# A two-layer attention block and a second block on one core: max rows as one-pass products, reciprocal spreads merged in pairs, and the second layer's context-key spread placed behind the third front tile

## The chip, the cores and the metric

The kernel runs on one core of one Trainium2 chip. The metric is the device time of one execution in microseconds (us); the median of three runs of the kernel before is 3325.97 us (3325.49 to 3326.18). Everything is float32 at the input and at the output.

## The reference, cut to what matters

Two blocks follow each other. The first (two layers, width 1024) has a main stream `x` of 512 tokens and a context stream of 256; the second block is left out here, since the change does not touch it.

```python
for l in range(2):
    zc = modulate(ctx_s, ...) @ w_in[l]
    qc, kc, vc = qkv_heads(zc, g_q[l], g_k[l])          # rms_norm over each head of 64
    z = modulate(x, ...) @ w_in[l]
    q, k, v = qkv_heads(z, g_q[l], g_k[l])
    q, k = apply_rope(q, cos, sin), apply_rope(k, cos, sin)
    k_all, v_all = concat(k, kc), concat(v, vc)         # 768 keys
    s = einsum(q, k_all) * 64 ** -0.5                   # 8 query heads, 2 key heads
    y_attn = softmax(s) @ v_all
    x = x + gt1 * merge_branches(z, y_conv, y_four, y_attn, ...)
    x = x + gt2 * sq_relu_mlp(...)
    if l == 0:                                          # the context's own attention, 256 keys
        yc_attn = gqa(qc, kc, vc); ctx_s = ctx_s + ...
```

In layer two the context stream is needed for its keys and values only.

## The kernel before, in words

**Weights.** Every weight comes from DRAM as a tile of 128 x 1024 float32 (512 KB) into one of four buffers `raw`, loaded by SyncE. ScalarE copies the tile into `w_hi` (type fp32r, L875), VectorE makes the rest `w_lo = raw - w_hi` (L2538). Both run three tiles ahead of TensorE (`LEAD`), with four buffers (`R`). On VectorE the making of `w_lo` for tile c + 3 stands in the same queue as the work on tile c, ahead of it (`lower_w` in `z_tile`).

**Products.** A product of full precision is three fp32r matmuls (`three`, L1644 to L1646: hi x hi, lo x hi, hi x lo). One front tile is 8 blocks of 3, so 24 matmuls of 128 x 512. A few small products have float32 operands instead of fp32r; each of these shows as two matmul records (and two weight loads) in the trace.

**Order.** The order of each engine's queue is the order of the code, written by hand; semaphores tie the engines together. The plan is: modulation, context stream of layer one (front, attention, merge, `w_o`, feed-forward), main stream of layer one, `kv_norm1` (keys and values of the context for layer two), main stream of layer two, then the second block.

**Max rows** (`max_row`, L1979). In an attention stage the largest score of each query is subtracted ahead of the exponential. VectorE reduces the scores of 128 queries to a column of 128 maxima, `mx` (L2839). For each head, TensorE turns these columns into one row with a product per 128 queries: weights are the column of `mx` (one column), moving is the identity of 128 columns; both are float32. A head has four such products in the main stream (512 queries) and two in the context stream (256). ScalarE reads the row (L1456), and the scores of the next head (`score_t`) wait for that. The stages have eight heads: the context of layer one, the main stream of layer one and that of layer two.

**Reciprocals** (`reciprocals_spread`, L2063). The denominators of the eight heads lie in rows 0, 32, 64 and 96 of two blocks of `scr`, four heads in each. In the merge stage each is spread over the 64 rows of its head: a float32 product with 64 weight columns for each head (a one at the head's row), two of them for the two halves of one bank. They are called in pairs of banks, behind merge tiles 0 and 1; so one call site issues four matmuls, with eight records. VectorE multiplies by each bank (L2915).

**Key norm of the context in layer two** (`kv_tail`). The context's keys are ready ahead of layer two's front. `front` first runs two tiles side by side (`abreast`), then `kv_tail`: sums of squares (L1811), the turned values (`v_turned`, L1765), and `head_spread` (L1792), which spreads the norm's factors over 128 rows and waits for them. These factors pass from ScalarE (root) to VectorE (reciprocal, L2673) and again to ScalarE (L1367, into `scr`). VectorE then multiplies the keys by the spread factors (L2684), copies them (L2690 to L2696), and goes on to the third front tile.

Of the kernel before, what the change touches and what calls it, by code (L numbers as in the profile page):

```python
# [7 lines left out]
F32R = mybir.dt.float32r  # L8
ALU = mybir.AluOpType
# [3 lines left out]
P = 128  # L13
# [3 lines left out]
CTX = 256  # L17
DEPTH = 2
HEAD = 64
# [364 lines left out]
def build(nc, ws, vecs, mats, ropes, x_in, ctx_in, bv_in, out, upto=None):  # L384
# [5 lines left out]
    with ExitStack() as stack:  # L390
        def sb(name, shape, dt=F32):
            return stack.enter_context(nc.sbuf_tensor(name, shape, dt))
# [15 lines left out]
        scr = sb("scr", [P, 4, SEQ])  # L408
# [4 lines left out]
        c_act = sb("c_act", [P, 16])  # L413
        c_parts = sb("c_parts", [P, KB, 4], F32R)
        pair = sb("pair", [4, 2])
        mx = sb("mx", [P, 2, 4])
        small = sb("small", [P, 64])
        eps = sb("eps", [P, 1])
        decay = sb("decay", [P, 4])
        unused_root = sb("unused_root", [P, 1])  # L420
        ones_r = sb("ones_r", [P, P], F32R)
        v_bias = sb("v_bias", [P, 8])
        o_bias = sb("o_bias", [P, 8])
        half_b = sb("half_b", [P, 8])
# [3 lines left out]
        bank = [stack.enter_context(nc.psum_tensor(f"bank{i}", [P, SEQ], F32)) for i in range(4, 8)]  # L428
        ring = stack.enter_context(nc.psum_tensor("ring", [P, R, SEQ], F32))

        ones, ident, head_ones, rot = (mat[:, i * P:(i + 1) * P] for i in range(4))
# [1207 lines left out]
        def _(pe):  # L1639
# [167 lines left out]
            def kv_tail(first):  # L1807

                pe.wait_ge(sq_ready, C.next(sq_ready))
                for tt in range(CTX // P):  # L1810
                    m = nc.tensor.matmul(bank[0][:, 2 * tt:2 * tt + 2], ctx_k_square[:, tt * P:(tt + 1) * P],  # L1811
                                         head_ones[:, 0:P:HEAD], start=True, stop=True)
                m.then_inc(ss_ready, 1)
                C.next(root_ready)
                v_turned("ctx", first + R)
                head_spread(0, CTX, False, 0, 0)
                C.next(lo_ready)

            def front(layer, stream, first):
                T, nf, main = length(stream), mix_tiles(stream), stream == "main"  # L1820
                k0, qn0, rot0 = C.now(lo_ready), C.now(s_qn) + (1 if layer else 0), C.now(s_rot_read)
                C.next(lo_ready, KB)

                def z_tile(c, before=None):
                    ready(c)
                    product(c, T, h_hi, h_lo, before=before)

                abreast(first, 2, T, k0)
                if layer:
                    kv_tail(first)  # L1830
                z_tile(first + 2)
                z_tile(first + 3)
                if layer:

                    pe.wait_ge(s_qn, C.next(s_qn))

                pe.wait_ge(lo_ready, C.next(lo_ready, 2))
                ready(first + 4)
                for tt in range(T // P):
                    s = slice(tt * P, (tt + 1) * P)  # L1840
                    for fb in range(2):
                        m = three(bank[tt][:, fb * 256:(fb + 1) * 256], y_hi[:, 2 + fb, s], y_lo[:, 2 + fb, s],
                                  *w(first + 4, 0, 256), True, True)
                m.then_inc(tile_done, 1)
                z_tile(first + 5)
                pe.wait_ge(lo_ready, C.next(lo_ready, T // P))
                half, nkt = T // 2, T // 2 // P
                per = TILE // half
                for parity in range(2):

                    at0 = parity * 2 * nkt
                    c = first + 6 + at0 // per
                    if at0 % per == 0:
                        ready(c)
                    for fb in range(2):
                        for idx in range(2 * nkt):
                            cs, kt = divmod(idx, nkt)
                            a = slice(fb * 256 + cs * P, fb * 256 + (cs + 1) * P)
                            b = 4 + parity * nkt + kt
                            m = three(bank[fb][:, parity * half:(parity + 1) * half], y_hi[:, b, a], y_lo[:, b, a],  # L1860
                                      *w(c, at0 % per + idx, half), idx == 0, idx == 2 * nkt - 1)
                    if parity or nf > 1:
                        m.then_inc(tile_done, 1)
                c = first + 6 + nf
                z_tile(c)

                pe.wait_ge(lo_ready, C.next(lo_ready, 2))
                head_sums(0, T)
                z_tile(c + 1)
                head_spread(0, T, main, qn0, rot0)  # L1870
                head_sums(1, T)
                z_tile(c + 2)
                head_spread(1, T, main, qn0, rot0)
                head_sums(2, T)
                z_tile(c + 3)
                head_spread(2, T, main, qn0, rot0)
                head_sums(3, T)
                z_tile(c + 4)
                head_spread(3, T, main, qn0, rot0)
                head_sums(4, T)  # L1880
                z_tile(c + 5)
                head_spread(4, T, main, qn0, rot0)
                z_tile(c + 6)
                z_tile(c + 7)
                C.next(s_qn, 5)

                pe.wait_ge(s_qn, C.now(s_qn))
                ready(c + 8)
                product(c + 8, T, h_hi, h_lo, o=bank[2][:, :T])

            def attention(layer, stream, first):
# [80 lines left out]
                def max_row(h):  # L1972

                    pe.wait_ge(s_max, C.next(s_max, nq))
                    if h >= 2:

                        pe.wait_ge(s_on, C.next(s_on, 2))
                    for qt in range(nq):
                        m = nc.tensor.matmul(bank[2 + h % 2][0:1, qt * P:(qt + 1) * P],  # L1979
                                             mx[:, h % 2, qt:qt + 1], ident, start=True, stop=True)  # L1980
                    m.then_inc(s_mrow, 1)

                def score_t(h, n):
# [74 lines left out]
            def reciprocals_spread(b, T):  # L2058
                if b % 2 == 0:
                    pe.wait_ge(s_recip, C.next(s_recip))  # L2060
                for i in range(2):
                    r = (2 * b + i) % 4 * 32
                    m = nc.tensor.matmul(bank[b][i * HEAD:(i + 1) * HEAD, :T],  # L2063
                                         ident[:, r:r + 1].to_broadcast([P, HEAD]), scr[:, 2 + b // 2, :T],
                                         start=True, stop=True)
                m.then_inc(s_spread, 1)

            def merge(stream, first):
                T = length(stream)
# [437 lines left out]
        def _(dve):  # L2507
            C = Counts()

            def step(ins, sem=dve_own):  # L2510

                ins.then_inc(sem, 1)
                dve.wait_ge(sem, C.next(sem))
# [1035 lines left out]
            dve.wait_ge(s_mat, 16)  # L3549
            step(nc.vector.tensor_tensor(pair[:, :], ident[0:4, 0:2], ident[0:4, 2:4], ALU.add), consts)  # L3550
            step(nc.vector.tensor_copy(ones_r[:, :], ones))

            dve.wait_ge(s_vec, 16)
            dve.wait_ge(s_lam, 1)
# [84 lines left out]
```

## Time and profile before

| what | value |
|---|---|
| median of three runs | 3325.97 us |
| time of the profiled execution | 3323.05 us |
| its span, first to last instruction | 3321.3 us |
| mean granted TensorE clock, as a share of 2.4 GHz | 0.987 |
| VectorE, ScalarE busy | 63%, 36% |
| moved from and to DRAM | 358 MB, mean 108 GB/s |
| the chain that ended last: TensorE, VectorE, ScalarE | 90%, 6%, 2% |

The span lies 1.75 us below the execution's own time; that execution lies 2.92 us below the median. A matmul record's duration contains latency that overlaps with the next matmul, so what a matmul costs is read from the distance between the starts of two that follow each other. In a row of the timeline the columns are: start in us, time in us that the merged instructions cover, engine, line, operation, output<-inputs, weights (rows*columns), output (rows x columns), count, and in brackets the engine's idle time ahead with what ended it.

### The profile page before, as it was taken

What the parts mean: (1) busy time and instruction counts of PE and PEld (TensorE: products, weight loads), DVE (VectorE), ACT (ScalarE), POOL (GpSimd) and SP (SyncE); (2) the same over time, 40 slices, a digit from 0 to 9 for tenths busy, and PEclk for the clock granted to TensorE, in tenths of its full rate; (3) what the DMA queues carried; (4) which work ended last, traced back from release to release, by engine and by line L of the source; (5) the groups of instructions that cost most, each with busy time, mean ns of one, the idle gap of its engine ahead of it and who ended that gap; (6) DMA issues with size and microseconds to landing.
All of it is one profiled execution on the core that took longest, in us unless ns stands there. A gap on an engine that the chain in (4) does not pass through costs nothing.

```text
span 3321.3 us, 43028 instructions
## 1 busy us (share of the span) xinstructions
PE 3239.8 (98%) x16209; PEld 2700.1 (81%) x16209; DVE 2096.4 (63%) x2914; ACT 1210.4 (36%) x1783; POOL 0.2 (0%) x4
## 2 busy tenths in 40 slices
PE   8999999999999999999999999999999999999998
PEld 5879997787888887878788888888888878888886
DVE  5777885655587778565466555785544576655446
ACT  3654444454232223344423222434222256542221
POOL 0000000000000000000000000000000000000000
PEclk9999999999999999999999999999999999999999
DMA  7554552211334454211122222231323336323222
GB/s 247 191 191 145 184 184 95 69 53 51 112 129 133 162 181 132 89 58 55 66 89 90 99 95 95 83 102 58 108 96 101 102 75 85 55 85 102 95 97 75
DMA packets 100717, 358.25 MB, mean 108 GB/s; under 512 B 11209, under 2 KB 12369, under 8 KB 100561
## 3 DMA queue, kind: packets, MB, share of 16 engines
q1 hardware_dynamic: 98864, 352.92, 31.9%
q10 hardware_dynamic: 1696, 3.16, 2.0%
q8 instruction: 109, 1.79, 0.2%
q14 instruction: 48, 0.39, 0.0%
HBM read 351.83 MB, written 2.10 MB: 107 GB/s over the span
## 4 chain that ended last, share of the span: by engine, by line
PE 90%; DVE 6%; ACT 2%; issue 1%; DMA 1%; DVEq 0%; ACTq 0%; SPq 0%
PE ring L1644 25%; PE ring L1645 25%; PE ring L1646 25%; PE bank L1644 2%; PE bank L1646 2%; PE bank L1645 2%; DVE w_lo L2538 1%; PE ring L1735 1%; ACT w_hi L875 1%; DMA raw<-ws 1%; PE ring L1968 1%; PE ring L1967 1%; PE bank L1992 1%; PE bank L1993 1%; PE ring L1938 1%
## 5 line engine op out<-in xcount | busy, mean ns | idle before, releaser
L1644 PE MATMUL ring<-h_hi,w_hi 128*128 128x512 f32 (+1 forms) x2776 | 1028.6, 371 | 21.1 <-DVE h_lo L2602 6.6
L1645 PE MATMUL ring<-h_lo,w_hi 128*128 128x512 f32 (+1 forms) x2776 | 1019.7, 367 | 0.0
L1646 PE MATMUL ring<-h_hi,w_lo 128*128 128x512 f32 (+1 forms) x2776 | 1019.3, 367 | 0.0
L2538 DVE TENSOR_TENSOR w_lo<-raw,w_hi 128x1024 fp32r<-128x1024 f32 x598 | 731.2, 1225 | 322.8 <-ACT w_hi L875 305.7
L875 ACT ACTIVATE w_hi<-raw 128x1024 fp32r<-128x1024 f32 x598 | 630.6, 1056 | 718.1 <-PE ring L1646 668.9
L1644 PEld LDWEIGHTS ring<-h_hi,w_hi 128*128 128x128 f32 x2776 | 528.8, 190 | 120.3 <-issue 28.5
L1646 PEld LDWEIGHTS ring<-h_hi,w_lo 128*128 128x128 f32 x2776 | 528.1, 190 | 86.0
L1645 PEld LDWEIGHTS ring<-h_lo,w_hi 128*128 128x128 f32 x2776 | 528.6, 190 | 82.4
L1644 PE MATMUL ring<-y_hi,w_hi 128*128 128x512 f32 (+1 forms) x1456 | 541.2, 372 | 10.4 <-DVE z L2817 7.8
L1645 PE MATMUL ring<-y_lo,w_hi 128*128 128x512 f32 (+1 forms) x1456 | 537.2, 369 | 0.0
L1646 PE MATMUL ring<-y_hi,w_lo 128*128 128x512 f32 (+1 forms) x1456 | 537.0, 369 | 0.0
L1644 PEld LDWEIGHTS ring<-y_hi,w_hi 128*128 128x128 f32 x1456 | 276.6, 190 | 60.4 <-DVE z L2817 10.7
L1646 PEld LDWEIGHTS ring<-y_hi,w_lo 128*128 128x128 f32 x1456 | 276.7, 190 | 45.8
L1645 PEld LDWEIGHTS ring<-y_lo,w_hi 128*128 128x128 f32 x1456 | 276.9, 190 | 44.2 <-issue 0.5
L1561 ACT ACTIVATE scr<-ring 128x512 f32<-128x512 f32 (+1 forms) x96 | 50.5, 526 | 302.5 <-PE ring L1646 300.0
L3033 DVE TENSOR_TENSOR z<-scr 128x512 f32<-128x512 f32 (+1 forms) x96 | 57.6, 600 | 125.1 <-ACT scr L1561 124.9
L2958 DVE SCALAR_TENSOR_TENSOR x<-ring,mod,x 128x512 f32<-128x512 f32 (+1 forms) x80 | 60.1, 751 | 118.3 <-PE ring L1646 118.2
L2849 DVE TENSOR_TENSOR y_lo<-z,y_hi 128x512 fp32r<-128x512 f32 (+1 forms) x112 | 72.3, 647 | 63.0 <-ACT y_hi L1472 61.6
L2839 DVE TENSOR_REDUCE mx<-ring 128x1 f32<-128x768 f32 (+1 forms) x80 | 67.9, 849 | 61.9 <-PE ring L1968 61.5
L1112 ACT ACTIVATE scr<-scr 128x512 f32<-128x512 f32 x40 | 25.3, 632 | 196.3 <-DVE scr L3326 196.3
L1472 ACT ACTIVATE y_hi<-bank 128x512 fp32r<-128x512 f32 (+1 forms) x112 | 63.4, 567 | 75.0 <-PE bank L1646 74.0
L1465 ACT ACTIVATE z<-bank 128x512 f32<-128x512 f32 (+1 forms) x112 | 63.6, 568 | 60.6 <-PE bank L1993 55.0
(369 smaller groups left out, 3136.8 us busy)
## 6 DMA issues: line engine op xcount, KB each, us to landing
raw<-ws SPq DMA_DIRECT2D x614, 512.0 KB, 3.3
z<-ws SPq DMA_DIRECT2D x48, 512.0 KB, 4.4
x<-x_t SPq DMA_DIRECT2D x1, 2048.0 KB, 12.1
out_t<-x SPq DMA_DIRECT2D x8, 256.0 KB, 2.0
z<-xc ACTq DMA_DIRECT2D x6, 256.0 KB, 11.3
xc<-ctx_t SPq DMA_DIRECT2D x1, 1024.0 KB, 7.7
z<-ropes ACTq DMA_DIRECT2D x2, 512.0 KB, 4.0
xc<-xc ACTq DMA_DIRECT2D x2, 256.0 KB, 11.2
```

The source lines that it names most:

```text
L875: nc.scalar.activation(w_hi[:, t % R, :], raw[:, t % R, :], ACT.Copy).then_inc(w_hi_ready, 1)
L1465: nc.scalar.activation(z[:, 13 + k % 2, :T], bank[k % 2][:, :T], ACT.Exp, scale=HEAD ** -0.5)\
L1472: nc.scalar.activation(y_hi[:, 4 + k % 2, :T], bank[k % 2][:, :T], ACT.Exp, scale=HEAD ** -0.5)\
L1561: nc.scalar.activation(scr[:, u % 2, :T], ring[:, c % R, :T], ACT.Relu).then_inc(evac, 1)
L1644: nc.tensor.matmul(o, a_hi, b_hi, start=start, stop=False)
L1645: nc.tensor.matmul(o, a_hi, b_lo, start=False, stop=False)
L1646: return nc.tensor.matmul(o, a_lo, b_hi, start=False, stop=stop)
L2538: nc.vector.tensor_tensor(w_lo[:, u, :], raw[:, u, :], f(w_hi[:, u, :]), ALU.subtract).then_inc(w_ready, 1)
L2839: nc.vector.reduce_max(mx[:, h % 2, qt:qt + 1], view[:, 0:n_kt * P], AX_X).then_inc(s_max, 1)
L2849: nc.vector.tensor_tensor(y_lo[:, b, :T], src, f(y_hi[:, b, :T]), ALU.subtract).then_inc(s_p, 1)
L2958: step(nc.vector.scalar_tensor_tensor(o, ring[:, c % R, :T], g, o, ALU.mult, ALU.add), post)
L3033: step(nc.vector.tensor_tensor(z[:, m % 2, :T], scr[:, m % 2, :T], scr[:, m % 2, :T], ALU.mult))
```

## The change

Three edits. First, `mx` is of type fp32r and is multiplied with an fp32r copy of the identity, `ident_r`. Second, a new constant `head_pick` has ones in 64 columns for each of the two heads of a bank, so that one product with 64 rows and 128 weight columns makes a whole bank: rows 0 to 63 for the even bank, rows 64 to 127 for the odd one. Third, `head_spread` leaves `kv_tail` and stands behind the third front tile of layer two. The two constants cost three VectorE instructions at the program's start.

```diff
-        mx = sb("mx", [P, 2, 4])
+        mx = sb("mx", [P, 2, 4], F32R)
...
+        ident_r = sb("ident_r", [P, P], F32R)
+        head_pick = sb("head_pick", [P, P])
...
                 v_turned("ctx", first + R)
-                head_spread(0, CTX, False, 0, 0)
                 C.next(lo_ready)
...
                 if layer:
                     kv_tail(first)
                 z_tile(first + 2)
+                if layer:
+                    head_spread(0, CTX, False, 0, 0)
                 z_tile(first + 3)
...
                         m = nc.tensor.matmul(bank[2 + h % 2][0:1, qt * P:(qt + 1) * P],
-                                             mx[:, h % 2, qt:qt + 1], ident, start=True, stop=True)
+                                             mx[:, h % 2, qt:qt + 1], ident_r[:, :], start=True, stop=True)
...
-                for i in range(2):
-                    r = (2 * b + i) % 4 * 32
-                    m = nc.tensor.matmul(bank[b][i * HEAD:(i + 1) * HEAD, :T],
-                                         ident[:, r:r + 1].to_broadcast([P, HEAD]), scr[:, 2 + b // 2, :T],
-                                         start=True, stop=True)
-                m.then_inc(s_spread, 1)
+                two = slice(b % 2 * HEAD, (b % 2 + 1) * HEAD)
+                nc.tensor.matmul(bank[b][:, :T], head_pick[two, :], scr[two, 2 + b // 2, :T],
+                                 start=True, stop=True).then_inc(s_spread, 1)
...
             step(nc.vector.tensor_copy(ones_r[:, :], ones))
+            step(nc.vector.tensor_copy(ident_r[:, :], ident))
+            for g in range(2):
+                step(nc.vector.tensor_tensor(head_pick[:, g * HEAD:(g + 1) * HEAD],
+                                             ident[:, 32 * g:32 * g + 1].to_broadcast([P, HEAD]),
+                                             ident[:, HEAD + 32 * g:HEAD + 32 * g + 1].to_broadcast([P, HEAD]), ALU.add))
```

TensorE's queue at the start of layer two's front, before. L1644 to L1646 are the matmuls of a product (behind the change L1646 to L1648), L1811 the sums of squares, L1765 the turned values, L1792 the spread.

```order
L1646 MATMUL ring<-h_hi,w_lo 128x512
L1811 MATMUL bank<-mat,z 128x2 x2
L1765 MATMUL bank<-mat,z 128x128 x2
L1792 MATMUL bank<-mat,scr 128x128 x2
L1644 MATMUL ring<-h_hi,w_hi 128x512
L1645 MATMUL ring<-h_lo,w_hi 128x512
```

The same place behind the change: the third tile's first matmuls follow the turned values.

```order
L1648 MATMUL ring<-h_hi,w_lo 128x512
L1813 MATMUL bank<-mat,z 128x2 x2
L1767 MATMUL bank<-mat,z 128x128 x2
L1646 MATMUL ring<-h_hi,w_hi 128x512
L1647 MATMUL ring<-h_lo,w_hi 128x512
```

And 24 rows on, where the third tile ends and the fourth begins, behind the change:

```order
L1647 MATMUL ring<-h_lo,w_hi 128x512
L1648 MATMUL ring<-h_hi,w_lo 128x512
L1794 MATMUL bank<-mat,scr 128x128 x2
L1646 MATMUL ring<-h_hi,w_hi 128x512
L1647 MATMUL ring<-h_lo,w_hi 128x512
```

The spread has moved behind the 24 matmuls of the third tile; nothing else of TensorE's queue moved there, and the queues of VectorE and ScalarE are the same as before at this place. TensorE's queue behind the first merge tile of layer one's main stream, before:

```order
L1645 MATMUL ring<-h_lo,w_hi 128x512
L1646 MATMUL ring<-h_hi,w_lo 128x512
L2063 MATMUL bank<-scr,mat 64x512 x4
L1644 MATMUL ring<-h_hi,w_hi 128x512
L1645 MATMUL ring<-h_lo,w_hi 128x512
```

and behind the change:

```order
L1647 MATMUL ring<-h_lo,w_hi 128x512
L1648 MATMUL ring<-h_hi,w_lo 128x512
L2065 MATMUL bank<-scr,head_pick 128x512 x2
L1646 MATMUL ring<-h_hi,w_hi 128x512
L1647 MATMUL ring<-h_lo,w_hi 128x512
```

Four products with 64 output rows became two with 128.

## Rows read from the trace of the kernel before

**Rows 1.** The page's first part: busy time, share of the span, instructions.
```profile
PE 3239.8 (98%) x16209; PEld 2700.1 (81%) x16209; DVE 2096.4 (63%) x2914; ACT 1210.4 (36%) x1783; POOL 0.2 (0%) x4
```

**Rows 2.** Timeline of TensorE, start of layer two's front.
```profile
1324.33 0.69 PE L1765 MATMUL bank<-mat,z 128*128 128x128 f32 x4
1330.01 1.23 PE L1792 MATMUL bank<-mat,scr 128*128 128x128 f32 x4 [4.99 <-ACT scr L1367]
...
1333.28 0.40 PE L1644 MATMUL ring<-h_hi,w_hi 128*128 128x512 f32 x1
...
1342.83 0.28 PE L1644 MATMUL bank<-w_hi,y_hi 128*128 128x256 f32 x1
...
1345.70 0.40 PE L1644 MATMUL ring<-h_hi,w_hi 128*128 128x512 f32 x1
```

**Rows 3.** Busy us by stretch (instructions), then granted clock, DMA share, GB/s.
```profile
108.00:245.00 137.00, 122.89 (x927) 106.82 (x927) 98.99 (x156) 82.55 (x147) 0.00 (x0) 0.95 0.60 202
640.00:760.00 120.00, 119.99 (x558) 96.31 (x558) 69.16 (x93) 58.78 (x96) 0.00 (x0) 1.00 0.16 53
1330.00:1333.00 3.00, 2.99 (x9) 2.60 (x10) 1.98 (x6) 1.17 (x2) 0.00 (x0) 0.52 0.12 44
```

**Rows 4.** Timeline of VectorE, the keys of the context in layer two.
```profile
1331.34 0.42 DVE L2684 TENSOR_TENSOR z<-z,bank 128x256 f32<-128x256 f32 x1 [0.66 <-PE bank L1792]
...
1334.28 1.23 DVE L2538 TENSOR_TENSOR w_lo<-raw,w_hi 128x1024 fp32r<-128x1024 f32 x1
```

**Rows 5.** Timeline of TensorE, first max row of layer one's main stream.
```profile
618.25 0.39 PE L1646 MATMUL ring<-h_hi,w_lo 128*128 128x512 f32 x1
618.57 1.03 PE L1979 MATMUL bank<-mat,mx 128*1 128x128 f32 x8
...
619.87 0.40 PE L1645 MATMUL ring<-h_lo,w_hi 128*128 128x512 f32 x1
```

**Rows 6.** Timeline of TensorE, short fp32r matmuls late in the program.
```profile
2749.78 0.22 PE L2363 MATMUL ring<-kv 128*128 128x128 f32 x1
2749.84 0.27 PE L2364 MATMUL ring<-kv 128*128 128x128 f32 x1
2749.95 0.45 PE L1644 MATMUL bank<-y_hi,w_hi 128*128 128x512 f32 x1
```

**Rows 7.** Timeline of TensorE, fp32r products with four weight columns begin.
```profile
124.24 0.28 PE L1646 MATMUL bank<-y_hi,kv 128*128 128x256 f32 x1
124.35 0.28 PE L1938 MATMUL ring<-w_hi,c_parts 128*4 128x256 f32 x1
```

**Rows 8.** Timeline of TensorE, first max row of the context stream.
```profile
109.80 0.60 PE L1979 MATMUL bank<-mat,mx 128*1 128x128 f32 x4
...
110.55 0.28 PE L1645 MATMUL ring<-h_lo,w_hi 128*128 128x256 f32 x1
```

**Rows 9.** Timeline of TensorE, float32 products with all 128 weight columns.
```profile
556.60 1.02 PE L1784 MATMUL bank<-z,mat 128*128 128x512 f32 x2
557.46 1.05 PE L1792 MATMUL bank<-mat,scr 128*128 128x128 f32 x8
558.35 0.51 PE L1772 MATMUL bank<-mat,scr 128*128 128x2 f32 x4
```

**Rows 10.** Timeline of TensorE, first reciprocals of layer one's main stream.
```profile
816.07 0.39 PE L1646 MATMUL ring<-h_hi,w_lo 128*128 128x512 f32 x1
816.39 1.94 PE L2063 MATMUL bank<-scr,mat 128*64 128x512 f32 x8
...
818.59 0.40 PE L1645 MATMUL ring<-h_lo,w_hi 128*128 128x512 f32 x1
```

**Rows 11.** Timeline of TensorE's weight loads, the same place.
```profile
816.87 0.14 PEld L2063 LDWEIGHTS bank<-scr,mat 128*64 128x64 f32 x2 [0.29 <-issue]
817.30 0.14 PEld L2063 LDWEIGHTS bank<-scr,mat 128*64 128x64 f32 x2 [0.28 <-issue]
```

**Rows 12.** Timeline of VectorE at the program's start.
```profile
26.14 1.22 DVE L2624 TENSOR_TENSOR z<-z 128x1024 f32<-128x1024 f32 x1 [9.69 <-ACT z L1319]
```

## The prediction

> **What bounds the kernel now.** I read the page's first part before anything else: TensorE is busy for 3239.8 of 3321.3 us, VectorE for 63%, ScalarE for 36% [rows 1]. So time is to be had in two ways: matmul time taken out where TensorE never rests, or an idle stretch of TensorE closed. The busy time by stretch then says which stage is which. From 640 to 760 us, inside the attention of layer one's main stream, TensorE is busy for 119.99 of 120 us at full clock while VectorE has 69 and ScalarE 59: there every us of matmul is a us of the kernel. From 108 to 245 us, the context's attention, it is busy for 122.9 of 137 us with VectorE at 99: there TensorE is only one of several links, and a part of what it saves is given back in waits [rows 3]. Last, the timeline at the start of layer two's front: an idle time of 4.99 us, TensorE waiting for ScalarE's copy of the key factors (L1367) [rows 2].
>
> **The third edit: the spread behind the third tile.** Before, the turned values start at 1324.33. Their four records are float32 with 128 columns, and eight such follow each other in 558.35 - 557.46 = 0.89 us, 0.11 each [rows 9]; so the third tile could start at 1324.77. What stands there instead is the spread at 1330.01, then the third and fourth tiles (48 matmuls, up to 1342.83) and the next tile's 24 matmuls of 256 columns, up to 1345.70 [rows 2]. From 1324.77 to 1345.70 is 20.93 us.
> After: the third tile waits for nothing that is late. The matmul at 1333.28 is the seventh of the 48, so the 42 steps to 1342.83 took 9.55, 0.2274 each; a tile at this pace is 5.46. The sum is 5.46 (third tile) + 0.45 (the spread, four records of 0.11) + 5.46 (fourth tile) + 2.87 (as now) = 14.24. Saved: 20.93 - 14.24 = 6.69. The idle time is 5.0 of it. The other 1.7 are a slow pace: between 1330 and 1333 the granted clock was 0.52 of 2.4 GHz, mostly the level of 1.2 GHz [rows 3], and before that TensorE had rested. With no rest there, I expect 2.4 GHz throughout.
> What is late next? The factors lie ready at about 1329.96 (the spread starts at 1330.01 [rows 2]), and the new spread starts at 1324.77 + 5.46 = 1330.23. So VectorE gets it at about 1331.4, as now (1331.34), and its `w_lo` for the tile three further on starts at 1334.28 as now [rows 4] and takes 1.23. TensorE then needs that `w_lo` at 1339.0 instead of 1345.7: slack 3.5 us. No DMA moves in SyncE's queue; the loads wait for `w_lo` and keep their times. I take 6.7. Bounds: 5.0, if only the idle time goes and the slow pace stays, and 6.9.
>
> **The first edit: max rows.** Main stream, before: from the start of the last ordinary matmul (618.25) to that of the second one behind the max row (619.87) are 1.62 us [rows 5]; two ordinary steps are 0.46, so a max row costs 1.16. Of that, eight records by 0.108 are 0.87, and 0.29 are gaps at the entry and the exit. After: four records, fp32r. The nearest rows are short fp32r matmuls of 128 columns, with 128 weight columns each: one follows 0.06 behind the other, and the next matmul 0.11 behind that, which is the pace at which such weights arrive [rows 6]. The weights here are one column, so I take 0.06, the pace of the moving columns: 4 x 0.06 = 0.24. As to the gaps: fp32r products with four weight columns begin 0.11 behind a 256-column matmul, without any gap [rows 7], and full-width float32 products begin without one too, the second group 0.86 behind the first for two records [rows 9]. The gap thus goes with float32 and few columns together, and should vanish. Saved: 1.16 - 0.24 = 0.92 for each of 8 heads x 2 stages, 14.7 us. Bounds: 0.64 each (10.2) with the gaps kept, 0.72 each (11.5) with 0.11 a record, 0.93 each (14.9) with 0.058.
> TensorEngine Tiling (Array Packing), section Tiling Modes, of the Trainium skill says that a change of tiling mode drains TensorE. By that rule a product of one weight column would be a tile of its own shape, fp32r or not, and the 0.29 would stay; rows 7 speak against it for fp32r.
> Context stream, before: 109.80 to 110.55 [rows 8], less two steps of 0.12, plus an entry gap of 0.09 as in rows 5, gives 0.60 to 0.72; for eight heads some 5.9 us (one of them runs at the half clock and costs 1.19). After: 2 x 0.06 each, with the slow one 1.0 in all. TensorE saves 4.9; as it idles for 14 of 137 us in this stage, waiting for chains over ScalarE and VectorE that in part start from TensorE's own tiles, I take 60%, 3.0. Bounds 0 and 4.9.
>
> **The second edit: reciprocals.** On paper two products become one. But the old ones already ran side by side. One full-width float32 product of 512 columns takes 0.86 for its two records, 0.43 each [rows 9]. Eight records of L2063 would be 3.4 us one after another; yet from 816.07 to 818.59 are 2.52, less 0.46 for two ordinary steps: 2.06, gaps of 0.34 included [rows 10]. The weight loads come in pairs 0.43 apart [rows 11]. So eight records took four steps of 0.43: the two halves of a bank, 64 columns each, shared the array.
> After, two products of 64 rows and 128 columns stand at a call, four records. In the array they lie in different rows, 0 to 63 and 64 to 127. If these share the array as the columns did, it is two steps: 0.86 + 0.34 = 1.20, saved 0.86. If not, four steps: saved nothing. There are four call sites in the main stream: 3.4 or 0. In the context (256 columns) half of it at two sites, 0.86, of which I keep 0.4, since the matmul behind it waits there for `w_lo` as well. I take 3.8: the nearest row, L2063 itself, shows that TensorE does run products on separate parts of the array at once. Bounds 0 and 4.3.
> TensorE: Matmul & The Clock Gate of the Trainium skill, section on packing small matmuls, gives 3.07x for four products of 32 rows each, so sharing by rows is a thing there; no row of this trace shows it. By the rule alone the term would be the same 3.4 to 4.3.
>
> **Start.** Three more VectorE instructions with fewer elements than the one of 0.42 us [rows 4], so under 1.3 us, are hidden by the 9.69 us that VectorE waits ahead of 26.14 [rows 12]. Cost 0; without that cover 1.3.
>
> **Sum.** 6.7 + 14.7 + 3.0 + 3.8 = 28.2. The profiled execution took 3323.05, 1.75 more than its span; 3323.05 - 28.2 = 3294.9. The median lies 2.92 higher: 3297.8, so 3298.
>
> **Rivals.**
> A. Products in separate rows do not run side by side. For it: no row shows rows sharing. Against: columns do. The second edit gives nothing: 24.4 saved, 3301.6.
> B. The gaps of the max row stay, because they belong to the one-column shape (the rule above), or a record costs 0.11. Against: rows 6 and 7. Main 10.2 to 11.5, context 1.5: 22.2 to 23.9 saved, 3302 to 3304.
> C. The chain binds in the context's attention, where a faster TensorE only waits longer; terms 3.0 and 0.4 go: 24.8 saved, 3301.2.
> D. Slower. The place is the two main attentions, the mechanism the clock. Each head's max row is now shorter, so TensorE comes earlier to products that wait for VectorE's or ScalarE's parts; a rest of some us went ahead of the 0.52 in rows 3. If such rests appeared once a head and left the clock at 1.2 GHz for half of the time, each us at that level would cost half a us. It decides from 2 x 28.2 = 56 us at the lower level; at 80 us of it the kernel would take 3298 + 40 = 3338. Against it: VectorE and ScalarE have half of their time free there, and TensorE rested for 0.01 of 120 us [rows 3].
>
> **How the numbers follow.** The forecast 0.62, A 0.16, B 0.09, C 0.09, D 0.02, and 0.02 for no change at all (the moved spread and the fp32r rows both hidden). The few stretches at the lower clock elsewhere may shift against the work by up to 3 us either way. Range: below, all terms at their best are 6.9 + 14.9 + 4.9 + 4.3 = 31.0, so 3295, less half of what the clock may give: 3293.5. Above, it holds A and C and most of B: 3304.5. A measurement of this kernel can tell about 0.2%, 6.7 us, from no change. Faster by more than that: 0.96; within: 0.02; slower: 0.02.
>
> **What would show it.** In the new profile: no wait of TensorE for L1367, the spread directly behind the third tile, and the granted clock at 1.0 from there. Max rows in four records 0.06 apart with no gap; if eight steps of time are still there or gaps of 0.1, B. Reciprocals: four records with two starts together and 0.43 between; four starts 0.43 apart, A. In the stretch of the context's attention, TensorE's idle time grows by less than 2 us; by 5, C. The forecast is wrong if the time lies above 3305 or below 3293.

## The result

The changed kernel takes 3295.53 us (median of four, 3294.24 to 3295.94); the kernel before, run beside it on the same chip, 3326.07 (3325.49 to 3328.72). The ratio is 0.991, interval 0.9898 to 0.9921: 30 us less, where 28.2 were worked out and 3298 was forecast. The profiled execution took 3295.76, its span 3294.0, against 3323.05 and 3321.3 before. So the two profiles are 27.3 us apart and the medians 30.5; the section on the reasons comes to that.

The page of the kernel after, first part, which answers to [rows 1]:

```profile
span 3294.0 us, 42823 instructions
PE 3215.2 (98%) x16105; PEld 2691.2 (82%) x16105; DVE 2096.2 (64%) x2917; ACT 1210.1 (37%) x1783; POOL 0.2 (0%) x4
```

TensorE lost 104 records (80 of the max rows, 24 of the reciprocals) and 24.6 us of busy time; the span fell by 27.3. Nothing else moved: VectorE has its three more instructions and the same busy time to 0.2 us.

**The spread.** Timeline of TensorE in the kernel after, the start of layer two's front, answering to [rows 2]:

```profile
1313.53 0.69 PE L1767 MATMUL bank<-mat,z 128*128 128x128 f32 x4
1313.98 0.48 PE L1646 MATMUL ring<-h_hi,w_hi 128*128 128x512 f32 x1
...
1319.52 0.60 PE L1794 MATMUL bank<-mat,scr 128*128 128x128 f32 x4
1319.88 0.48 PE L1646 MATMUL ring<-h_hi,w_hi 128*128 128x512 f32 x1
...
1325.41 0.28 PE L1646 MATMUL bank<-w_hi,y_hi 128*128 128x256 f32 x1
...
1328.29 0.40 PE L1646 MATMUL ring<-h_hi,w_hi 128*128 128x512 f32 x1
```

No idle time stands in it. The third tile starts 0.45 behind the turned values, the spread 5.54 later, the fourth tile 0.36 behind that, and the place that lay at 1345.70 lies at 1328.29. From the turned values to it are 14.76 us instead of 21.37: 6.6 less. Busy time by stretch, 22 us from the same point of the program on, first before, then after (columns as in [rows 3]):

```profile
1324.00:1346.00 22.00, 17.01 (x87) 14.63 (x86) 11.47 (x23) 7.65 (x14) 0.00 (x0) 0.92 0.32 106
```

```profile
1313.00:1335.00 22.00, 22.00 (x121) 19.10 (x120) 15.77 (x28) 11.71 (x20) 0.00 (x0) 1.00 0.41 139
```

The 5 us of rest are gone and the granted clock is 1.00 (2.4 GHz) in place of 0.92. VectorE has its turn a little earlier than forecast, answering to [rows 4]: 0.71 behind the spread's start, and 6.70 behind the start of the turned values, where 7.1 were forecast.

```profile
1320.23 0.42 DVE L2684 TENSOR_TENSOR z<-z,bank 128x256 f32<-128x256 f32 x1 [0.34 <-PE bank L1794]
```

**The max rows.** Timeline of TensorE after, the first max row of the main stream, answering to [rows 5]:

```profile
617.67 0.39 PE L1648 MATMUL ring<-h_hi,w_lo 128*128 128x512 f32 x1
617.90 0.40 PE L1982 MATMUL bank<-ident_r,mx 128*1 128x128 f32 x4
618.13 0.44 PE L1646 MATMUL ring<-h_hi,w_hi 128*128 128x512 f32 x1
618.41 0.40 PE L1647 MATMUL ring<-h_lo,w_hi 128*128 128x512 f32 x1
```

The row starts 0.23 behind a 512-column matmul, which is that matmul's ordinary step, so there is no gap at the entry; the next product starts 0.23 behind the row, so there is none at the exit. One thing is new: the product behind it takes a step of 0.28 instead of 0.23. By the same sum as before, 618.41 - 617.67 = 0.74, less two steps of 0.23, leaves 0.28 (0.29 in finer figures) for this row, which cost 1.16. Over the 16 rows of the two main stages, the same stretch takes 0.74 to 0.76 after and 1.62 to 1.63 before: 0.87 less for each.

**The reciprocals.** Timeline of TensorE after, the first call of the main stream, answering to [rows 10]:

```profile
808.45 0.39 PE L1648 MATMUL ring<-h_hi,w_lo 128*128 128x512 f32 x1
808.77 1.13 PE L2065 MATMUL bank<-scr,head_pick 64*128 64x512 f32 x4
809.83 0.50 PE L1646 MATMUL ring<-h_hi,w_hi 128*128 128x512 f32 x1
810.16 0.39 PE L1647 MATMUL ring<-h_lo,w_hi 128*128 128x512 f32 x1
```

810.16 - 808.45 = 1.71, less 0.46: 1.25, where it was 2.05. Four records of 0.43 one after another would be 1.72 alone, so the two halves of 64 rows do run at once. The four starts lie in pairs, as the records of L2065 in four short stretches show (length, busy time and, in brackets, the number of records in it, then clock, DMA share and GB/s):

```profile
808.76:808.79 0.03, 0.02 (x2) 1.00 0.00 0
808.79:809.29 0.50, 0.50 (x2) 1.00 0.31 82
809.29:809.32 0.03, 0.03 (x4) 1.00 0.00 0
```

Two records start within 0.03 us (at 808.768 and 808.775 in the trace), the other two start together 0.53 later. Before, the pairs of column halves followed each other 0.43 apart. The entry kept its gap: 0.32 from the matmul ahead to the first record, where that matmul's step is 0.23.

**The context's attention.** Busy time by stretch after, the stretches of [rows 3]:

```profile
108.00:245.00 137.00, 121.91 (x913) 109.33 (x912) 99.63 (x156) 82.87 (x147) 0.00 (x0) 0.93 0.61 202
630.00:750.00 120.00, 119.99 (x555) 98.53 (x554) 70.70 (x95) 61.70 (x101) 0.00 (x0) 1.00 0.17 57
```

In the main attention TensorE is as full as before. In the context's, though, the profile shows no gain at all: from the first max row to the first reciprocals are 134.94 us, and 135.06 before. The granted clock between 108 and 245 us was 0.93 in place of 0.95. That was the open question, and most experiments bear on it.

### The profile page after: what moved, and what is told of

It reads as the page before. It is cut to its first block, busy times and chain, and to the rows that moved or that the text cites. A ratio compares the mean times of both kernels' runs of the same rounds, so it can differ in the third digit from the quotient of the medians.

```text
span 3294.0 us, 42823 instructions
## 1 busy us (share of the span) xinstructions
PE 3215.2 (98%) x16105; PEld 2691.2 (82%) x16105; DVE 2096.2 (64%) x2917; ACT 1210.1 (37%) x1783; POOL 0.2 (0%) x4
## 4 chain that ended last, share of the span: by engine, by line
PE 90%; DVE 6%; ACT 2%; issue 1%; DMA 1%; DVEq 0%; ACTq 0%; SPq 0%
PE ring L1646 25%; PE ring L1648 25%; PE ring L1647 25%; PE bank L1646 2%; PE bank L1648 2%; PE bank L1647 2%; DVE w_lo L2538 1%; DMA raw<-ws 1%; ACT w_hi L877 1%; PE ring L1737 1%; PE ring L1971 1%; PE ring L1970 1%; PE bank L1995 1%; PE bank L1996 1%; PE ring L1941 1%
## 5 line engine op out<-in xcount | busy, mean ns | idle before, releaser
L1646 PE MATMUL ring<-h_hi,w_hi 128*128 128x512 f32 (+1 forms) x2776 | 1028.8, 371 | 21.9 <-DVE h_lo L2602 12.0
L1648 PE MATMUL ring<-h_hi,w_lo 128*128 128x512 f32 (+1 forms) x2776 | 1020.1, 367 | 0.0
L1646 PEld LDWEIGHTS ring<-h_hi,w_hi 128*128 128x128 f32 x2776 | 529.5, 191 | 116.0 <-issue 25.0
L1648 PEld LDWEIGHTS ring<-h_hi,w_lo 128*128 128x128 f32 x2776 | 529.1, 191 | 86.0
L1646 PE MATMUL ring<-y_hi,w_hi 128*128 128x512 f32 (+1 forms) x1456 | 540.0, 371 | 10.3 <-DVE z L2817 7.5
L1648 PE MATMUL ring<-y_hi,w_lo 128*128 128x512 f32 (+1 forms) x1456 | 536.5, 368 | 0.0
L1646 PEld LDWEIGHTS ring<-y_hi,w_hi 128*128 128x128 f32 x1456 | 275.9, 189 | 59.4 <-DVE z L2817 10.1
L1648 PEld LDWEIGHTS ring<-y_hi,w_lo 128*128 128x128 f32 x1456 | 275.7, 189 | 45.6
L2839 DVE TENSOR_REDUCE mx<-ring 128x1 fp32r<-128x768 f32 (+1 forms) x80 | 67.9, 849 | 62.0 <-PE ring L1971 61.5
```

Of the source, the lines that this page charges most:

```text
L1646: nc.tensor.matmul(o, a_hi, b_hi, start=start, stop=False)
L1648: return nc.tensor.matmul(o, a_lo, b_hi, start=False, stop=stop)
L2839: nc.vector.reduce_max(mx[:, h % 2, qt:qt + 1], view[:, 0:n_kt * P], AX_X).then_inc(s_max, 1)
```

## The experiments

The runs of each job share their own runs of the kernel before, with medians of 3324.34 (21 runs), 3325.00 (18) and 3325.12 (15).

The edits are shown shortened: arguments are left out (`...`), and so are the constants `ident_r` and `head_pick` with the VectorE instructions that make them, which each run has where it uses them.

**One edit at a time.** Each kernel is the one before with one of the three edits.

> The first edit alone (max rows in fp32r, the rest as before). My theory: in the main attentions the edit is worth 0.87 us for each of 16 heads, 13.9 us in all, and in the context's attention about nothing (the after trace shows TensorE there 1.7 us ahead and then back to 0.0). So the time is 3326 - 14 = 3312. Rival (the prediction's term): the context's attention gives 3 us more, 3309.

```
-   matmul(bank[2 + h % 2][0:1, ...], mx[:, h % 2, qt:qt + 1], ident)
+   matmul(bank[2 + h % 2][0:1, ...], mx[:, h % 2, qt:qt + 1], ident_r[:, :])   # mx in fp32r
```

Measured 3309.55 (3308.3 to 3311.09), ratio 0.9955 (0.9941 to 0.9968): 14.8 less. It is about half of the gain. That is nearer to the rival's 3309 than to the theory's 3312, but the interval (10.6 to 19.6 us) holds both.

> The second edit alone (one product of 64 rows for each bank). Theory: two products in rows 0 to 63 and 64 to 127 run side by side, 0.80 us saved at each of four main call sites, so 3.2 us, and with two sites in the context 3.6: 3322.4. Rival: they save nothing by themselves, and what the trace of the changed kernel gave there came from something else: 3326.

```
-   for two heads: matmul(bank[b][64 rows of it], mat, scr[...])
+   matmul(bank[b][:, :T], head_pick[two, :], scr[two, 2 + b // 2, :T])
```

Measured 3318.44 (3314.32 to 3323.1), ratio 0.9983 (0.9974 to 0.9992), 5.9 less by the medians. The call takes the same 1.25 us in its timeline as in the changed kernel. Four calls times 0.80 are 3.2, and the context's two calls 0.4 each at most; the interval (2.7 to 8.6 us) holds the 3.6 to 4.0, and the runs of this kernel are 8.8 us apart. In its profile, 5.2 us shorter than that of before, the four calls give 3.2, and two places where the clock stood low for less time give 1.6 each; the section on the reasons shows these two places.

> The third edit alone (the spread behind the third tile of layer two). Theory: the idle time of 5.0 us and the slow pace of 1.7 us behind it both go: 6.7 saved, 3319.3, and no half-clock stretch near 1330 us. Rival: only the idle time goes and the clock falls somewhere else: 3321.

```
-   head_spread(...); z_tile(first + 2); z_tile(first + 3)
+   z_tile(first + 2); head_spread(...); z_tile(first + 3)
```

Measured 3317.27 (3313.18 to 3323.77), ratio 0.998 (0.9971 to 0.9989): 7.1 less. The three alone make 14.8 + 5.9 + 7.1 = 27.8; together they gave 30. They add up within the scatter.

**Are the context's max rows worth anything?** The changed kernel with the old float32 rows in the context alone:

> The changed kernel, but the eight max rows of the context's attention are float32 products again (two records each); the 16 of the main streams stay fp32r. Theory: the context's attention is bound by chains and by stretches at the lower clock, so its eight faster rows give back nothing: as the changed kernel within 1 us, 3295.5. Rival: they are worth the predicted 3 us or more, and a clock stretch that fell badly hid it: 3298.5.

```
+   col = mx[:, h % 2, qt:qt + 1]
-   matmul(..., mx[:, h % 2, qt:qt + 1], ident_r[:, :])
+   matmul(..., col if main else col.bitcast(F32), ident_r[:, :] if main else ident)
```

Measured 3296.54 (3294.41 to 3299.34), ratio 0.9918 (0.9905 to 0.9932), against the changed kernel's 0.991. By the time alone they are one; that agrees with rows worth nothing, and with rows worth 3 as well. Its trace tells more: its stage took 134.84 us at a granted clock of 0.96, while the changed kernel had the same length at 0.92. I therefore ran both kernels again, to see what the clock does to this stage when the code is the same.

> The changed kernel once more, beside the others on one chip. Theory: what differs from one execution to the next is how long TensorE's clock stands at 1.2 GHz behind the same rests; in the context's attention the stage takes 132.5 us with 10 us at that level and 136.6 with 20. The sum of the times at the lower level and the span move together, half a us for each us. Rival: the stage takes 136.6 us whatever the clock.

Measured 3294.83 (3289.87 to 3296.87), ratio 0.991 (0.9895 to 0.9925).

> The kernel before once more, for a second profile. Theory: its context's attention takes 136.7 us with 10 to 14 us at the lower level and 140.6 with 20. Rival: 136.8 whatever the clock.

Measured 3326.31 (3323.2 to 3328.12), ratio 1.0 (0.999 to 1.001).

The same program, twice. Busy time by stretch of the changed kernel, first execution: from the first max row to the first reciprocals, and a part of it.

```profile
109.89:244.83 134.94, 119.85 (x895) 107.29 (x892) 97.77 (x153) 81.51 (x144) 0.00 (x0) 0.92 0.61 202
110.00:140.00 30.00, 24.84 (x173) 22.23 (x171) 19.70 (x33) 16.54 (x31) 0.00 (x0) 0.85 0.65 222
```

The same of its repeat:

```profile
109.06:239.80 130.74, 115.69 (x895) 103.35 (x892) 97.69 (x153) 81.29 (x144) 0.00 (x0) 0.96 0.63 208
110.00:140.00 30.00, 24.94 (x200) 21.97 (x200) 21.49 (x39) 17.66 (x31) 0.00 (x0) 1.00 0.67 226
```

The number of TensorE's records is the same, 895, and the stage is 4.2 us shorter. Between 110 and 140 us the engine was busy for as long (24.84 and 24.94), but did 173 records in one execution and 200 in the other, because in the first a part of them ran at 1.2 GHz. Both executions rest at the same place (next fences), so the rest goes before the low clock in one of them and doesn't in the other. The repeat of the changed kernel, TensorE's timeline:

```profile
117.23 0.39 PE L1970 MATMUL ring<-kv,y_hi 128*128 128x256 f32 x1 [3.39 <-DVE y_lo L2791]
```

and its first execution:

```profile
118.24 0.58 PE L1970 MATMUL ring<-kv,y_hi 128*128 128x256 f32 x1 [3.56 <-DVE y_lo L2791]
```

The matmul behind the rest takes 0.58 at the one level and 0.39 at the other. With this, each run's stage can be set beside its clock. From the first max row to the first reciprocals, in us, for every profile without filling matmuls; each column has the granted clock of that stretch and, from the trace's record of the granted level, the us at 1.2 GHz in it:

| context's rows | 0.96 (10.2 us) | 0.95 (13.7 us) | 0.94 (17.1 us) | 0.93 to 0.92 (20.5 us) |
|---|---|---|---|---|
| float32 | 134.79, 134.84 | 135.06 (before) | 137.23, 137.97 (before, again) | 138.84, 137.78 (128 weight columns) |
| fp32r | 130.74 (changed, again), 131.06 (128 weight columns) | | | 134.94 (after), 134.81, 135.25 |

With rows of one weight column, the two kinds are 134.8 and 130.7 at 0.96, and 138.8 (one execution) and 135.0 at the low end: the fp32r rows save 3.8 to 4.1 us of this stage at either clock, and 10.3 us more at 1.2 GHz cost it 4.0 to 4.2, so 0.4 for each, as the theory for the repeat had it (4.1 for 10 us). Single executions leave this line: the first profile of before lies 1.1 below it, the two at 0.94 within 0.5 of it. My theory for the experiment with float32 rows, that they give nothing, falls. The profile's silence was a gain of 4 against 6.8 us more at the lower level, worth some 3, and some 1 us by which the first profile of before was short and for which no run shows a cause.

**Filling the rest.** If the low clock behind that rest costs up to 4 us, work without a use in the rest might keep it away. Forty matmuls of 256 columns whose result nobody reads go behind the second score tile of the context's preamble:

> The changed kernel with 40 matmuls without use (256 columns, into a free bank) where TensorE rests for some 6 us at the start of the context's attention. Theory: the stretch at the lower clock behind that rest goes, and the stage takes about 133 us, 3 to 4 us less than in the profile of the changed kernel; the time is 3293 or below. Rival: the matmuls delay the work behind them and the clock falls at a later rest, 3296 or more.

```
    score_t(0, 1)
+   if not main:
+       for _ in range(40):
+           matmul(bank[2][:, :T], ones_r[:, :], h_hi[:, 0, :T], start=True, stop=True)
```

Measured 3292.78 (3291.83 to 3293.19, four runs), ratio 0.9902 (0.9887 to 0.9917), 2.0 below the changed kernel's repeat of the same job. The same with the context's rows in float32:

> The same with float32 max rows in the context's attention. Theory: with the same clock on both sides the eight fp32r rows show their worth there, 4 us: 137 us for the stage, 3297. Rival (rows hidden behind other chains): the same as the run before it within 1 us.

Measured 3298.22 (3294.95 to 3301.08), ratio 0.9917 (0.9903 to 0.993): 5.4 above its sister, where the rows should be worth 4, and no run of the one lies among those of the other. That points the same way, though the clock was not the same on both sides (0.94 and 0.96 in the stage), and the intervals of the two ratios overlap. Busy time by stretch, with fp32r rows:

```profile
108.94:240.78 131.84, 120.18 (x935) 107.95 (x933) 97.72 (x153) 81.19 (x144) 0.00 (x0) 0.96 0.61 207
110.00:140.00 30.00, 28.34 (x232) 25.77 (x232) 21.31 (x38) 17.02 (x31) 0.00 (x0) 1.00 0.62 214
```

and with float32 rows:

```profile
110.00:140.00 30.00, 28.39 (x230) 25.50 (x229) 20.59 (x34) 16.59 (x30) 0.00 (x0) 1.00 0.63 215
109.56:247.27 137.71, 126.69 (x951) 110.97 (x950) 97.70 (x153) 81.13 (x144) 0.00 (x0) 0.94 0.59 197
```

In both, the stretch from 110 to 140 us ran at 2.4 GHz. The second fell to 0.94 later in the stage, so a filled rest does not hold the clock for the whole of it. And without any filling the repeat above had 1.00 there too, and a faster stage by 1.1 us. Two things speak for the filling. One is what followed the rest: of the twelve profiles without it, all with a rest of 3.0 to 5.1 us at this place, eleven have the lower level behind it and only that repeat has not; with it, neither of two has. The other is the spread of the times: 1.4 us over four runs against 7.0 for the changed kernel. It is the fastest kernel by its median, but the intervals of the two ratios overlap (0.9887 to 0.9917, 0.9895 to 0.9925) and the float32 pair showed no gain from it (0.9917 against 0.9918). So it keeps the clock up at this place, but whether it helps the time stays open.

**What makes the gaps and the pace of a max row?** Two things changed at once: the type, and with it the number of records. The number of weight columns stayed at one. First the kernel before with the same column repeated 128 times as weights (rows 1 to 127 of the output are not used):

> The kernel before, with the column of maxima repeated to 128 weight columns in the float32 max rows (the row is made 128 times, only the first is read). Theory: the 0.29 us of gaps ahead of and behind a max row belong to float32 products with few weight columns, so they go: eight records of 0.11, 0.89 and some 0.05 at the end, about 0.93 instead of 1.16 for a head, 3.7 us saved over 16 heads: 3322. Rival: the gaps come with float32 or with the wait for VectorE, and stay: 3326.

```
-   matmul(bank[2 + h % 2][0:1, ...], mx[:, h % 2, qt:qt + 1], ident)
+   matmul(bank[2 + h % 2][:, ...], mx[:, h % 2, qt:qt + 1].to_broadcast([P, P]), ident)
```

Measured 3317.92 (3315.01 to 3322.08), ratio 0.9977 (0.9967 to 0.9987): 7 us less than before, with 128 times the weights. The timeline of TensorE at its first max row:

```profile
623.59 0.39 PE L1646 MATMUL ring<-h_hi,w_lo 128*128 128x512 f32 x1
623.82 1.05 PE L1979 MATMUL bank<-mat,mx 128*128 128x128 f32 x8
624.63 0.48 PE L1644 MATMUL ring<-h_hi,w_hi 128*128 128x512 f32 x1
624.94 0.39 PE L1645 MATMUL ring<-h_lo,w_hi 128*128 128x512 f32 x1
```

The gap at the entry is gone (623.82 - 623.59 = 0.23), and 1.35 - 0.46 = 0.89 remain of 1.16. Over the 16 main rows that is 4.3 us; the context's eight give some 2 more by the same sum (0.28 or 0.18 each), and the 7.1 of the medians hold both with their interval of 4.3 to 11. The same with fp32r:

> The changed kernel, with the column of maxima repeated to 128 weight columns in the fp32r max rows. Theory: the pace is then that of the weights, 0.11 a record, so a row costs 0.29 + 3 x 0.05 = 0.45 to 0.5 instead of 0.29: 3 us slower over 16 heads than the changed kernel, 3298.5. Rival: the records stay 0.06 apart, 3295.5.

Measured 3294.65 (3291.0 to 3299.82), ratio 0.991 (0.9894 to 0.9927). The timeline:

```profile
614.18 0.39 PE L1648 MATMUL ring<-h_hi,w_lo 128*128 128x512 f32 x1
614.40 0.56 PE L1982 MATMUL bank<-ident_r,mx 128*128 128x128 f32 x4
614.80 0.45 PE L1646 MATMUL ring<-h_hi,w_hi 128*128 128x512 f32 x1
615.08 0.39 PE L1647 MATMUL ring<-h_lo,w_hi 128*128 128x512 f32 x1
```

0.90 - 0.46 = 0.44 for a row instead of 0.29. So 128 weight columns are the dearer choice in fp32r and the cheaper one in float32. The 16 x 0.16 = 2.5 us that this would cost don't show in the time (its profile had the good clock of 0.96 in the context), so the timeline decides here, not the median.

**Is it the rows that share the array?** The second edit alone, with picks of the full height of 128 rows in place of 64:

> The second edit alone, with picks of all 128 rows (zeros in the other half), so that the two products of a call site use the same part of the array. Nothing else differs from the run with the second edit alone. Theory (sharing by rows is what pays): four records one after another, 0.43 apart, 1.7 us and little gap, about 1.8 for a call site against 1.25 with 64 rows and 2.05 before; over four sites 1 us saved instead of 3.2. Rival (fewer records pay, not sharing): as with 64 rows, two steps.

```
-   matmul(bank[b][:, :T], head_pick[two, :], scr[two, 2 + b // 2, :T])
+   matmul(bank[b][:, :T], head_pick[:, b % 2, :], scr[:, 2 + b // 2, :T])
```

Measured 3323.06 (3319.56 to 3324.93), ratio 0.9993 (0.9983 to 1.0002): no gain that can be told from none. The timeline:

```profile
818.12 0.39 PE L1647 MATMUL ring<-h_hi,w_lo 128*128 128x512 f32 x1
818.35 1.88 PE L2062 MATMUL bank<-scr,head_pick 128*128 128x512 f32 x4
819.66 0.79 PE L1645 MATMUL ring<-h_hi,w_hi 128*128 128x512 f32 x1
820.29 0.39 PE L1646 MATMUL ring<-h_lo,w_hi 128*128 128x512 f32 x1
```

2.17 - 0.46 = 1.71 for a call: between 2.05 before and 1.25 with 64 rows. No gap stands at its entry, so of the 0.80 that the edit saves 0.34 come with full-size records as well, and 0.46 only from the sharing.

**Where is the best place for the spread?** One tile further, behind the fourth:

> The changed kernel, with the spread of the key factors one tile later, behind the fourth front tile. Theory (slack of 3.5 us on VectorE's side): the spread starts 5.5 us later, VectorE's keys and the w_lo behind them too; TensorE waits for the keys' norm and for that w_lo, 2.2 us together, and the time is 3297.7. Rival: where the spread stands does not matter once the third tile is ahead of it: 3295.5.

```
    z_tile(first + 2)
-   head_spread(...)
    z_tile(first + 3)
+   head_spread(...)
```

Measured 3296.19 (3294.54 to 3299.4), ratio 0.9909 (0.9892 to 0.9926). The timeline:

```profile
1325.43 0.60 PE L1794 MATMUL bank<-mat,scr 128*128 128x128 f32 x4
1326.62 0.38 PE L1646 MATMUL bank<-w_hi,y_hi 128*128 128x256 f32 x1 [0.58 <-DVE z L2684]
...
1330.36 0.50 PE L1646 MATMUL ring<-h_hi,w_hi 128*128 128x512 f32 x1 [0.61 <-DVE w_lo L2538]
```

The next tile now starts 1.19 behind the spread instead of 0.45 or less, after a wait for VectorE's product of the spread, and a second wait, for the `w_lo` that VectorE makes later, follows, as the theory said. From the matmul behind the front's first wait to the first max row of the attention are 114.47 us (from 1301.03) against 112.72 in the changed kernel (from 1300.54), with 3.4 us at 1.2 GHz in both: 1.7 lost, where the theory had 2.2. Two tiles behind are one too many; the median, 1.4 above the repeat in another job, can't show it.

## Why the prediction was right

**The third edit**, 6.7 taken, 6.6 to 6.7 measured. The wait went, no other took its place, and the clock stayed at 2.4 GHz from there. The profile of the spread alone has the same 22 us full at 1.00.

**The first edit, main rows**, 14.7 taken, 0.87 x 16 = 13.9 measured. The gaps vanished and the records came 0.06 apart, as worked out. The size was off by 0.05 a row: I had priced the moving columns of the row only, and the product behind it takes a step of 0.28 where 0.23 is ordinary. A likely cause, which no run isolates: the weights of that product begin to load only 0.06 ahead of it, behind a short record, where 0.22 is ordinary. It isn't the row's shape, since the step is 0.28 behind the row with 128 weight columns too.

**The first edit, context rows**, 3.0 taken, 3.8 to 4.1 measured at equal clock. The term held two sizes that were off, and they partly cancel. At 2.4 GHz a context row takes 0.56 or 0.50 us less than before (three matmul starts, 0.96 to 0.40 or 0.85 to 0.35), so the eight save TensorE 4.3 and not 4.9; and not 60% of that reaches the end but about 90%. The bounds held it; the first profile alone would have made it 0.

**The second edit**, 3.8 taken, 3.2 in the main stream, and in the context 1.21 to 0.83 for each of two calls, so up to 0.8 more. The main calls give 0.80 and not 0.86. The two records of a pair start together, as forecast, but the second pair follows 0.53 behind the first and not 0.43. Rival A, that separate rows don't run side by side, is out by the call's own 1.25. TensorE: Matmul & The Clock Gate of the Trainium skill, section on packing small matmuls, says that matmuls in separate tiles of the array run concurrently, some 4 ns from start to start. The traces agree for two groups of 64 rows in float32: the starts of a pair are 7 ns apart, and a call takes 1.25 against 1.71 at full height.

**Rival B**, gaps that belong to the one-column shape, is out by the changed kernel, and the experiments with wide weights say why it looked likely: in float32 the entry gap does go with the few columns (0.23 in place of 0.32 to the row when they are 128). TensorEngine Tiling (Array Packing) of the Trainium skill, section Tiling Modes, says that a change of mode drains TensorE. If a product of fewer rows or columns is such a change, the float32 products here fit that (an entry gap of 0.09 with 1 or 64 weight columns and with 64 rows, none at full size), and the fp32r ones don't: a one-column row has neither gap. Rival B's own sum had a slip: with 0.11 a record it saves 6.7 + 11.5 + 1.5 + 3.8 = 23.5, not 23.9: 3302.5.

**Rival C**, a chain that binds in the context, is out at equal clock. The sign named for it points the same way in the two first profiles: TensorE's idle time between 108 and 245 us grew by 1.0, from 14.1 to 15.1, under the 2 named. **Rival D**, a loss by the clock in the main attentions, is out: 119.99 of 120 us busy at 1.00 there.

**The sum.** 6.7 + 13.9 + 3.9 + 3.2 + 0.4 to 0.8 are 28 to 28.5, against 28.2 forecast and 27.3 between the two spans. That the sum came out this close is in part luck: the main rows and the reciprocals' main calls were 1.0 below their terms, the context's rows about 1 above theirs. The forecast for the profiled execution was 3294.9, and it took 3295.76. The 2.5 us between 3298 and the median of 3295.53 are a term that wasn't about the change: I added the 2.92 by which the profiled execution of before lay under its median. After the change it lies 0.2 above. The repeats show that this offset is chance: two profiles of one kernel are 3294.0 and 3288.1 in span, those of the other 3321.3 and 3326.3. The part of this that I could trace is the clock. Without the first 100 us and the last 20, the one profile of the changed kernel has 58.0 us at 1.2 GHz, the other 44.4. The 13.6 us less are 10.2 in the context's attention and 3.4 near 2850 us; matmul by matmul, the repeat gains 4.2 at the first place and 1.6 at the second, of the 5.9 in the span. Two such stretches also explain why the spans of before and after agree with the sum although the context's gain didn't show. Busy time by stretch before:

```profile
1035.00:1050.00 15.00, 15.00 (x70) 12.86 (x69) 13.17 (x17) 5.43 (x8) 0.00 (x0) 0.77 0.35 110
2245.00:2260.00 15.00, 15.00 (x72) 12.73 (x71) 3.75 (x8) 4.34 (x8) 0.00 (x0) 0.77 0.00 1
```

and after, at the same places of the program:

```profile
1027.00:1042.00 15.00, 15.00 (x77) 12.77 (x76) 14.55 (x20) 5.02 (x7) 0.00 (x0) 0.89 0.42 141
2222.00:2237.00 15.00, 14.83 (x78) 12.48 (x77) 5.36 (x11) 7.37 (x13) 0.00 (x0) 0.89 0.00 0
```

Each low stretch is 3.4 us shorter and gives 1.4 to 1.6 us: 3 us that stand in no term of the sum, against the 4 that the context did not show. I had allowed 3 us either way; 5 to 6 would have been right for two single executions (5.0 and 5.9 between the two profiles of each kernel). The medians, 30.5 apart, leave some 2 us above the sum. The kernel before has medians from 3324.3 to 3326.3 in its five sets of runs, so that is within what they can tell. But chance is not shown to be all of it: both profiles of before have 6.8 us at 1.2 GHz at each of the two places, and both of the changed kernel 3.4, so these 3 us may belong to the kernels as they stand. Two profiles of each can't settle it.

## What to carry to other kernels

Before a small term is read off two profiles, run one of the kernels twice and set each stage beside its granted clock: here the same code gave 134.94 and 130.74 us, as much as the term. A short product between long ones costs more than its columns. Its gaps hang on the type and the shape together, so in float32 a full-width product can be cheaper than a narrow one, and in fp32r the narrow one is. Where two products of float32 use half of the rows each, put them in separate rows.

## What the runs showed of the hardware that was not expected

- Float32 with 128 identical weight columns beats float32 with one: 0.89 against 1.16 us for eight records of 128 moving columns. In fp32r it is the other way, 0.44 against 0.29 for four.
- A rest of 3.6 us at one place of a program is followed by the level of 1.2 GHz in one execution (granted clock 0.85 between 110 and 140 us), and one of 3.4 us at the same place not in another (1.00). Over all twelve profiles with that rest, eleven fell.
- Two float32 products in separate halves of the rows take 1.25 us with their gaps where two of full height take 1.71, so float32 too shares the array by rows. The two start 7 ns apart, but the step to the next pair is 0.53 us, where pairs that share by columns step by 0.43.
